# Norms between two engines, ScalarE tables requested ahead of waits, and pooling handed over bank by bank, in a two-block fp32 model kernel

## The chip, the core and the metric

The kernel runs on one core of a Trainium2 chip. TensorE multiplies matrices into the eight banks of PSUM, VectorE (DVE) and ScalarE (ACT) work on tiles in SBUF and PSUM, GpSimd (POOL) helps in the second block, and SyncE (SP) issues the transfers of the weights. The metric is the time of one execution on the device in microseconds; lower is better.

## What is computed

A batch of one, 256 tokens of 1024 fp32 numbers, passes a two-layer block and then a second block. Cut to the parts around the change:

```python
def rms_norm(x, g, eps=1e-6):
    return x * rsqrt(mean(x * x, -1) + eps) * g

# first block
h = h + even_mixer(rms_norm(h, ln_mix_even), ...)   # differential attention + gated recurrence
h = h + swiglu(rms_norm(h, ln_ffn_even), ...)       # hidden width 2816
h = h + pool_mixer(rms_norm(h, ln_mix_odd), pool_w, pool_scale)   # windows 2, 4, 8, 16
h = h + moe_swiglu(rms_norm(h, ln_ffn_odd), ...)    # 8 experts of 3584, top 2
x = rms_norm(h, final_g)

# second block: mod_* are six vectors from the condition c, ctx a second sequence of 256 tokens
hx = rmsnorm(x, g_mix) * (1 + mod_x[1]) + mod_x[0]
hc = rmsnorm(ctx, g_mix) * (1 + mod_c[1]) + mod_c[0]
x = x + mod_x[2] * hybrid_mixer(hx, hc, ...)        # gated delta net and a gated recurrence in two directions
hx = rmsnorm(x, g_ffn) * (1 + mod_x[4]) + mod_x[3]
x = x + mod_x[5] * hier_moe(hx, ...)                # 4 groups of 8 experts of 512, top 2 in the best group
out = rmsnorm(x, g_final)
```

## The kernel before

Every engine has its own program, written out in order, and they meet at semaphores: `done(...)` counts a semaphore up at the end of an instruction and makes the same engine wait for it, `wait_ge(*at(name, n))` waits for the n-th signal of that name. The order of each engine is the order of the code. Names such as `poolT_copied` or `gates_ready` share one semaphore with others of their stage (the table SHARED), which is why the order below shows `ve_mixer1` or `pe_hgrn2`.

The 256 tokens are two tiles of 128 (t = 0, 1), held in `res[:, t, :]` with tokens on the partitions. For projections the features must be on the partitions: TensorE transposes 16 blocks of 128x128 of the scaled rows `xn` into four PSUM banks (`norm_T`), each bank with two of the eight feature chunks for all 256 tokens, and the banks are copied to `hTx`.

There are nine norms, numbered 0 to 8: before the mixer (0), the FFN (1), pooling (2), of the context (3), before the first experts (4), final of block one (5), before the second mixer (6), before the second experts (7), and the output (8). In each, ScalarE squares the two token tiles with a running sum (`sumsq`), VectorE divides and adds eps (`ms_ready`), ScalarE computes exp(-0.5 ln(ms)) in two instructions that need two different activation tables (`rstd_ready`), and VectorE scales both tiles into `xn` (L1309, `xn_ready`). For norms 5 and 8 VectorE multiplies by the gain row as a second pass (L1647, L1950). After the transposes VectorE empties the banks: `norm_copy` (L1315, norms 0, 1, 4) with one 128x512 multiply a bank, `norm_modulate` (L1325, norms 3, 6, 7) with one 128x256 multiply-add for each chunk.

A ScalarE function needs its table in place. In the kernel before no load is written in the code; the compiler puts an ACT_TABLE_LOAD directly ahead of the first instruction of another table. Where that instruction waits for two semaphores, one of the two waits moves onto the load.

Pooling (L959 to L973): TensorE multiplies the rows of norm 2 with a band matrix into banks 0 to 3 (one signal `pool_ready`), VectorE copies them with a gain (L1610, `poolT_copied`), TensorE multiplies with `pool_w` (`pool_y`), VectorE multiplies by `pool_scale` (L1617) and adds to `res` (L1621).

The large weights stream through a ring of six slots of 2 MB on SyncE's queue, in the order of `plan`; each load waits until the slot's last reader is done. The first experts (`units_round`) work in 56 units of up, transpose and down (L705, L712, L726), the second (`pairs_round`) in 16 pairs of experts (L790, L806). Here a load of the next pair waits for `m2_g`, `m2_u` and `m2_dn` of the one before.

In the second mixer, L1201 and the lines behind it are one direction of the gated recurrence (d = 0, 1): ScalarE's sigmoids, VectorE's preparation (L1814 to L1820), Ln on ScalarE, VectorE's running sums (L1828), Exp on ScalarE, TensorE's transposes of the decayed keys, ScalarE's copy of them to `kdTok`, the product for the state, VectorE's copy of it (L1841), and then eight levels in which all engines hand on. In front of norm 7 VectorE adds the mixer's output to `res` (L1906, L1908), makes eight diagonal matrices (L1911, `dg_ready`), and a one-element memset (L1913) signals `res_ready`. For that signal GpSimd waits too: it then issues the loads of the router's columns and biases (L2353 to L2356), for which TensorE waits ahead of the router product (`router2_in`, all four).

## Time and profile before

| what | value |
|---|---|
| median of 3 runs | 2769.88 us (2763.08 to 2772.87) |
| profiled execution | 2766.34 us, its span 2764.5 us |
| TensorE busy | 2476.4 us, 90% of the span |
| VectorE, ScalarE, GpSimd busy | 631.5, 369.1, 150.4 us |
| table loads on ScalarE | 65, 83.4 us together |
| moved by the weights' queue | 666.91 MB |

The span by stages:

| stretch, us | stage | TensorE busy, us | granted clock | DMA share |
|---|---|---|---|---|
| 0 to 176 | norm 0, projections, attention | 126.9 | 0.88 | 0.72 |
| 176 to 218 | recurrent gates, output projection | 29.6 | 0.84 | 0.55 |
| 218 to 231 | norm 1 | 3.9 | 0.61 | 0.44 |
| 231 to 458 | FFN | 227.0 | 1.00 | 0.33 |
| 458 to 537 | norms 2 to 4, pooling, routing | 38.0 | 0.68 | 0.37 |
| 537 to 1521 | first experts | 967.7 | 0.99 | 0.95 |
| 1521 to 1551 | norms 5 and 6, context keys | 21.1 | 0.89 | 0.51 |
| 1551 to 1856 | projections and delta net | 270.5 | 0.94 | 0.00 |
| 1856 to 2192 | gated recurrence, branches, output | 298.8 | 0.97 | 0.25 |
| 2192 to 2237 | norm 7, routing | 17.9 | 0.66 | 0.43 |
| 2237 to 2740 | second experts | 472.2 | 0.98 | 0.98 |
| 2740 to 2764.5 | norm 8, store | 2.7 | 0.62 | 0.12 |

The granted clock is the share of TensorE's full 2.4 GHz that it ran at, so 0.5 is 1.2 GHz. In the rows of the timeline the first number is the start, the second how long, and the bracket at the end names how long the engine was idle before and what released it.

### The profile page before, as it was taken

The page shows a single profiled execution, that of the slowest core. Times are in us where ns is not written, and L with a number is a line of the kernel's source. Part 1 is how long each engine was busy: PE and PEld are TensorE (multiplying, and loading weights), DVE is VectorE, ACT ScalarE, POOL GpSimd, SP SyncE. Part 2 cuts the span into 40 slices and gives each one's busy share as a digit, 9 for nine tenths or more (in the row PEclk, how much of TensorE's full clock was granted, in tenths as well). Part 3 has the DMA queues.
Part 4 walks back from the last instruction along what each step waited for, and adds up shares of the span by engine and source line. Part 5 has one row for each costly group of instructions (what it writes and reads, how often), then busy time and mean ns, then how long its engine had stood idle before and what let it go on. Part 6 is the DMA issues. An engine that isn't in the chain of part 4 may idle for free.

```text
span 2764.5 us, 52752 instructions
## 1 busy us (share of the span) xinstructions
PE 2476.4 (90%) x24386; PEld 1594.9 (58%) x24386; DVE 631.5 (23%) x1191; ACT 369.1 (13%) x596; POOL 150.4 (5%) x140
## 2 busy tenths in 40 slices
PE   6768998599999999999999879999789879999996
PEld 5536775456556656655566658895567534443442
DVE  1441001401010100100010346741542232222223
ACT  1121001100000000000000232312241101011011
POOL 1000000000000000000000005530210000000000
PEclk9889999799999999999999989999999989999998
DMA  8574332399989999998999200013021449999994
GB/s 290 183 273 145 131 137 87 116 393 352 393 309 393 351 355 344 351 394 313 393 351 367 84 1 1 1 44 139 31 92 61 161 186 399 399 399 402 402 398 166
DMA packets 273243, 676.24 MB, mean 245 GB/s; under 512 B 5875, under 2 KB 9422, under 8 KB 268814
## 3 DMA queue, kind: packets, MB, share of 16 engines
q1 hardware_dynamic: 270608, 666.91, 64.3%
q0 software_dynamic: 2112, 6.04, 0.6%
q8 instruction: 184, 3.01, 0.4%
q14 instruction: 21, 0.17, 0.0%
q10 hardware_dynamic: 318, 0.10, 0.0%
HBM read 671.98 MB, written 1.05 MB: 243 GB/s over the span
## 4 chain that ended last, share of the span: by engine, by line
PE 59%; DMA 10%; DVE 5%; ACT 3%; issue 2%; SPq 2%; POOL 1%; DVEq 0%; ACTq 0%
PE ps L705 21%; PE ps L615 14%; PE ps L726 11%; DMA ring<-in_w_exp_up 10%; PE ps L790 5%; ACT arena L1956 2%; SPq L562 2%; PE ps L1074 1%; PE ps L1086 1%; PE ps L1084 1%; PE ps L712 1%; PE ps L688 1%; POOL arena L2348 1%; ACT L1956 1%; PE ps L806 1%
## 5 line engine op out<-in xcount | busy, mean ns | idle before, releaser
L705 PE MATMUL ps<-ring,arena 128*32 128x256 f32 x10752 | 597.8, 382 | 16.9 <-issue 15.6
L705 PEld LDWEIGHTS ps<-ring,arena 128*32 128x32 f32 x10752 | 349.0, 111 | 249.7 <-issue 32.3
L615 PE MATMUL ps<-hT,ring 128*128 128x256 f32 (+1 forms) x1792 | 443.9, 409 | 22.2 <-ACT arena L1956 7.3
L615 PEld LDWEIGHTS ps<-hT,ring 128*128 128x128 f32 x1792 | 346.9, 194 | 124.7 <-issue 69.4
L1956 ACT ACTIVATE arena<-ps 128x384 f32<-128x384 f32 (+5 forms) x311 | 165.2, 552 | 1826.6 <-PE ps L705 576.2
L726 PE MATMUL ps<-ring,arena 128*32 128x256 f32 x5376 | 300.5, 379 | 0.0
L790 PE MATMUL ps<-ring,arena 128*64 128x512 f32 x1024 | 235.2, 614 | 31.7 <-DMA ring<-in_w_exp_up 28.8
L726 PEld LDWEIGHTS ps<-ring,arena 128*32 128x32 f32 x5376 | 173.9, 110 | 115.3 <-issue 1.3
L1403 DVE TENSOR_TENSOR arena<-arena,ps 128x384 f32<-128x384 f32 x56 | 31.0, 554 | 825.3 <-ACT arena L1956 825.3
L790 PEld LDWEIGHTS ps<-ring,arena 128*64 128x64 f32 x1024 | 81.0, 141 | 182.7 <-issue 182.7
L615 PE MATMUL ps<-arena 128*128 128x128 f32 (+1 forms) x1048 | 132.2, 287 | 20.6 <-DVE arena L1431 7.5
L615 PEld LDWEIGHTS ps<-arena 128*128 128x128 f32 x1048 | 128.6, 203 | 22.5 <-DVE arena L1431 7.6
L806 PE MATMUL ps<-ring,arena 128*64 128x512 f32 x512 | 113.4, 595 | 0.0
L2292 POOL TENSOR_TENSOR arena<-arena,table 128x512 f32<-128x512 f32 x24 | 32.1, 1355 | 1442.1 <-ACT arena L1956 1415.3
L1956 ACT ACT_TABLE_LOAD x65 | 83.4, 1283 | 197.6 <-PE ps L615 84.7
L1454 DVE TENSOR_TENSOR arena<-arena,ps 128x512 f32<-128x512 f32 x16 | 11.0, 687 | 303.8 <-PE ps L790 303.8
L954 PE MATMUL ps<-ring,arena 128*128 128x512 f32 x176 | 79.0, 592 | 0.0
L1956 ACT ACTIVATE arena<-arena 128x512 f32<-128x512 f32 (+3 forms) x72 | 59.5, 864 | 137.2 <-DVE arena L1662 32.2
L806 PEld LDWEIGHTS ps<-ring,arena 128*64 128x64 f32 x512 | 35.3, 137 | 66.6 <-issue 66.6
L615 PE MATMUL ps<-ring,arena 128*128 128x512 f32 (+2 forms) x176 | 61.2, 502 | 12.3 <-DVE arena L1309 9.7
L646 PE MATMUL ps<-table,arena 128*128 128x128 f32 x96 | 20.0, 396 | 57.4 <-DVE arena L1309 57.4
L777 PE MATMUL ps<-arena 128*128 128x512 f32 x136 | 62.9, 605 | 1.1 <-ACT arena L1956 1.1
(353 smaller groups left out, 1808.0 us busy)
## 6 DMA issues: line engine op xcount, KB each, us to landing
ring<-in_moe_wg SPq DMA_DIRECT2D x56, 2048.0 KB, 11.4
ring<-in_moe_wu SPq DMA_DIRECT2D x56, 2048.0 KB, 16.4
ring<-in_moe_wd SPq DMA_DIRECT2D x56, 2048.0 KB, 17.2
ring<-in_w_exp_gate SPq DMA_DIRECT2D x32, 2048.0 KB, 17.5
ring<-in_w_exp_up SPq DMA_DIRECT2D x32, 2048.0 KB, 18.8
ring<-in_w_exp_down SPq DMA_DIRECT2D x32, 2048.0 KB, 15.0
ring<-in_w_in SPq DMA_DIRECT2D x13, 2048.0 KB, 10.7
ring<-in_w_ada SPq DMA_DIRECT2D x12, 2048.0 KB, 10.5
```

The source lines that it names most:

```text
L562: sp.dma_start(dst, w[2 * p + j, :, :].rearrange(rows_, p=P))\
L615: last = mm(outp, l, r, start=(i == 0), stop=(i == n - 1))
L688: last = mm(ps[:, 4 + q, t * S:(t + 1) * S], un_GcT[32 * q:32 * q + 32, 1 - b, 3 * t + r, :], ysb[32 * q:32 * q + 32, r * S:(r + 1) * S], ...
L705: last = mm(flat[32 * q:32 * q + 32, S * r:S * r + S], x_[:, k, 32 * r:32 * r + 32], gu[:, :, k, q * P:(q + 1) * P], start=(k == 0), stop= ...
L726: last = mm(flat[32 * q:32 * q + 32, 3 * 512 + S * r:3 * 512 + S * r + S], un_actT[:, c, r, :], d_[:, c, q * S:(q + 1) * S], start=(j == 0 ...
L777: last = mm(ps[:, (6 if t == 0 else 4) + c, :], GcT[:, 1 - b, t, :], ysb[:, c * 512:(c + 1) * 512], start=True, stop=True)
L790: last = mm(ps[64 * j:64 * j + 64, part, :], x_[:, k, 64 * j:64 * j + 64], weights(3 * j + part, KC)[:, k, :], start=(k == 0), stop=(k == ...
L806: last = mm(ps[64 * j:64 * j + 64, 4 + h_, :], pr_actT[:, c, 64 * j:64 * j + 64], weights(3 * j + 2, 4)[:, c, h_ * 512:(h_ + 1) * 512], st ...
L954: last = mm(ps[:, 4 + 2 * t + c, :], actb[:, (n - 1) % 4, t * P:(t + 1) * P], d_[:, j, c * 512:(c + 1) * 512], start=(n == 1), stop=(n == ...
L1403: V.tensor_tensor(un_act, un_sg, up_, ALU.mult).then_inc(inc("m1_act"), 1)
L1956: return nc.scalar.activation(*a, **k)
L2292: G.tensor_tensor(WK[g][d][2 + l % 2], WK[g][d][1], rep(level_mask(l, d == 0), 4), ALU.mult)\
```

## The change

Six things change.

- **Loads are written out.** `functions(names)` issues a table load at a chosen place, 27 in all, none inside a loop. Mostly it stands right behind the last instruction of the table before and ahead of the next wait. The compiler still adds a load wherever the table in place is not the one needed, so Exp behind Ln keeps its own. Two of them stand ahead of a plain copy: Ln before `mod_rows` in the attention, Exp before the copy to `kdTok` in the second direction.
- **Squares start at the first tile.** `res_half` signals that tile 0 of `res` is complete, and the square of tile 0 waits for that alone. In front of norm 8 and after norm 5 VectorE works tile by tile for this.
- **Scaling is shared.** VectorE scales tile 0, ScalarE tile 1 (`xn_act`); TensorE waits for both. In norms 5 and 8 VectorE scales and multiplies by the gain in one pass per tile (`norm_result`), and the output is stored tile by tile.
- **Transposed banks are shared.** VectorE empties banks 0 and 2, ScalarE banks 1 and 3 (`gained`, `hT_act`, `hTc_act`).
- **Pooling is signalled bank by bank**, four signals each for `pool_ready`, `poolT_copied` and `pool_y`; TensorE's second product runs group by group instead of tile by tile, and VectorE finishes the first half of the columns before the second.
- **In front of norm 7** the eight diagonal matrices move ahead of the wait for the output projection, and the memset goes.

```diff
@@ SyncE, end @@
-            sp.wait_ge(*at("result", 1))
-            sp.dma_start(out[0].rearrange("(t p) d -> p t d", p=P), res[:, :, :]).then_inc(inc("out_stored"), 16)
-            sp.wait_ge(*at("out_stored", 16))
+            for t in range(NT):
+                sp.wait_ge(*at("result", t + 1))
+                sp.dma_start(out[0, t * P:(t + 1) * P, :], res[:, t, :]).then_inc(inc("out_stored"), 16)
+            sp.wait_ge(*at("out_stored", 16 * NT))
@@ TensorE, pooling @@
-            last.then_inc(inc("pool_ready"), 1)
-            pe.wait_ge(*at("poolT_copied", 1))
+                if c % 2:
+                    last.then_inc(inc("pool_ready"), 1)
             w = take("poolw")
-            for t in range(NT):
-                for g in range(4):
+            for g in range(4):
+                pe.wait_ge(*at("poolT_copied", g + 1))
+                for t in range(NT):
                     last = chain(ps[:, 4 + 2 * t + g // 2, (g % 2) * S:(g % 2 + 1) * S],
                                  [(poolT[:, 2 * g + k, t * P:(t + 1) * P], w[:, 2 * g + k, :]) for k in range(2)])
-            last.then_inc(inc("pool_y"), 1)
+                last.then_inc(inc("pool_y"), 1)
@@ VectorE, norms @@
-                for t in range(NT):
-                    last = V.tensor_scalar(xn[:, t, :], src[:, t, :], rstd[:, t:t + 1], None, ALU.mult)
-                done(last, "xn_ready")
+                done(V.tensor_scalar(xn[:, 0, :], src[:, 0, :], rstd[:, 0:1], None, ALU.mult), "xn_ready")
+            def norm_result(i, row, names):
...
+                for t in range(NT):
+                    done(V.scalar_tensor_tensor(res[:, t, :], res[:, t, :], rstd[:, t:t + 1], row, ALU.mult, ALU.mult), names[t])
             def norm_copy(i, gain):
-                for b in range(4):
+                for b in (0, 2):
...
-                for c in range(KC):
+                for c in (0, 1, 4, 5):
@@ VectorE, in front of norm 7 @@
+            for c in range(8):
+                last = V.tensor_scalar(dg2[:, c, :], ident, mod[:, 40 + c, 0:1], None, ALU.mult)
+            done(last, "dg_ready")
             ve.wait_ge(*at("grow_ready", 1))
...
-            for c in range(8):
-                last2 = V.tensor_scalar(dg2[:, c, :], ident, mod[:, 40 + c, 0:1], None, ALU.mult)
-            done(last2, "dg_ready")
-            done(V.memset(lams[:, 7:8], 0.0), "res_ready")
+                    if n and t == 0:
+                        last.then_inc(inc("res_half"), 1)
+            done(last, "res_ready")
@@ ScalarE @@
+            def functions(names):
+                nc.scalar.preload_act_table_set(names)
+            def norm(i, src, needs, scaled=True):
                 for t in range(NT):
+                    ac.wait_ge(*at(*needs[t]))
                     last = act(xn[:, t, :], src[:, t, :], ACT.Square, accum_out=ss[:, t:t + 1])
                 done(last, "sumsq")
                 ac.wait_ge(*at("ms_ready", i + 1))
                 done(act(lnv, ms, ACT.Ln))
                 done(act(rstd, lnv, ACT.Exp, scale=-0.5), "rstd_ready")
+                if scaled:
+                    act(xn[:, 1, :], src[:, 1, :], ACT.Copy, scale=rstd[:, 1:2]).then_inc(inc("xn_act"), 1)
+            def gained(dst, gain, name, shift=None):
+                for b in (1, 3):
+                    ac.wait_ge(*at("xnT_ready", 4 * nT[0] + b + 1))
+                    for c in (2 * b, 2 * b + 1):
+                        x_, g_ = ps[:, b, (c % 2) * S:(c % 2 + 1) * S], gain[:, c:c + 1]
+                        if shift is None:
+                            last = act(dst[:, c, :], x_, ACT.Copy, scale=g_)
+                        else:
+                            last = act(dst[:, c, :], x_, ACT.Identity, scale=g_, bias=shift[:, c:c + 1])
...
+            functions(SIG)
             ac.wait_ge(*at("gelu_in", 1))
...
+            functions(EXP)
             ac.wait_ge(*at("log_a", 1))
...
+            functions("sqrt_and_others")
             ac.wait_ge(*at("one_minus", 1))
...
-            norm(1)
+            functions(LN)
+            norm(1, res, [("res_half", 1), ("res_ready", 1)])
+            gained(hTx, colA("ln_ffn_even", 0, 8), "hT_act")
+            functions(SILU)
...
+            functions(LN)
             ac.wait_ge(*at("hTc_ready", 1))
-            norm(4, res, ("res_ready", 3))
+            norm(4, res, [("res_half", 3), ("res_ready", 3)])
...
                     done(act(gd0, ps[:, 6:8, :].rearrange("p b (h q) -> p (b h) q", h=2), ACT.Sigmoid), "gate_sig")
+                    functions(EXP)
                 ac.wait_ge(*at("kdT_ready", d + 1))
```

ScalarE from the square root of the recurrent gates to the FFN. `ve_mixer1`, `res_ready`, `res_half`, `ms_ready` are VectorE's signals, `ac_mixer1`, `sumsq`, `ac_step`, `rstd_ready` its own, `xnT_ready` and `gu_ready` TensorE's. Before:

```order
L1956 ACTIVATE arena,small<-res 128x1024 [waits res_ready,ac_mixer1]
L1956 ACTIVATE arena,small<-res 128x1024
L1956 ACT_TABLE_LOAD [waits ms_ready]
L1956 ACTIVATE small<-small 128x2 [waits sumsq]
L1956 ACT_TABLE_LOAD
L1956 ACTIVATE small<-small 128x2 [waits ac_step]
L1956 ACT_TABLE_LOAD [waits gu_ready]
L1956 ACTIVATE arena<-ps 128x256 [waits rstd_ready]
```

Now:

```order
L1981 ACT_TABLE_LOAD [waits ac_mixer1]
L1973 ACTIVATE arena,small<-res 128x1024 [waits res_half]
L1973 ACTIVATE arena,small<-res 128x1024 [waits res_ready]
L1973 ACTIVATE small<-small 128x2 [waits ms_ready,sumsq]
L1973 ACT_TABLE_LOAD
L1973 ACTIVATE small<-small 128x2 [waits ac_step]
L1973 ACTIVATE arena<-res,small 128x1024 [waits rstd_ready]
L1973 ACTIVATE hT<-ps,pA 128x256 [waits xnT_ready]
L1973 ACTIVATE hT<-ps,pA 128x256
L1973 ACTIVATE hT<-ps,pA 128x256 [waits xnT_ready]
L1973 ACTIVATE hT<-ps,pA 128x256
L1981 ACT_TABLE_LOAD
```

The load with the wait for the mean is gone from between the squares and Ln and stands ahead of the squares; the scaling of one tile and four chunks of the transposed banks have come to ScalarE.

TensorE in pooling: the band product and the product with `pool_w`. `ve_mixer1` is VectorE's copy of the pooled banks, `loaded1` and `loaded2` the two weights. Before:

```order
L615 MATMUL ps<-ring,arena 128x256 [waits loaded1,xn_ready]
L615 MATMUL ps<-ring,arena 128x256 x15
L615 MATMUL ps<-ring,arena 128x256 [waits loaded2,ve_mixer1]
L615 MATMUL ps<-ring,arena 128x256 x15
L646 MATMUL ps<-table,arena 128x128 [waits xn_ready]
```

Now:

```order
L616 MATMUL ps<-ring,arena 128x256 [waits loaded1,xn_act,xn_ready]
L616 MATMUL ps<-ring,arena 128x256 x15
L616 MATMUL ps<-ring,arena 128x256 [waits ve_mixer1,loaded2]
L616 MATMUL ps<-ring,arena 128x256 x3
L616 MATMUL ps<-ring,arena 128x256 [waits ve_mixer1]
L616 MATMUL ps<-ring,arena 128x256 x3
L616 MATMUL ps<-ring,arena 128x256 [waits ve_mixer1]
L616 MATMUL ps<-ring,arena 128x256 x3
L616 MATMUL ps<-ring,arena 128x256 [waits ve_mixer1]
L616 MATMUL ps<-ring,arena 128x256 x3
```

One wait for all four banks has become a wait for each, ahead of four products.

ScalarE in the second direction of the gated recurrence, from the sigmoid of the gates to the first levels. The copy of 128x1024 into arena is that to `kdTok`. Before:

```order
L1956 ACT_TABLE_LOAD [waits pe_hgrn2]
L1956 ACTIVATE hT<-ps 128x4x256 [waits ac_hgrn2]
L1956 ACTIVATE arena<-ps 128x1024 [waits pe_hgrn2,ac_hgrn2]
L1956 ACT_TABLE_LOAD [waits Wd_ready]
L1956 ACTIVATE arena<-arena 128x512 [waits ac_hgrn2]
```

Now:

```order
L1973 ACT_TABLE_LOAD [waits pe_hgrn2]
L1973 ACTIVATE hT<-ps 128x4x256 [waits ac_hgrn2]
L1981 ACT_TABLE_LOAD [waits ac_hgrn2]
L1973 ACTIVATE arena<-ps 128x1024 [waits pe_hgrn2]
L1973 ACTIVATE arena<-arena 128x512 [waits Wd_ready,ac_hgrn2]
```

The load for Exp and the copy to `kdTok` have changed places.

## Rows read from the trace of the kernel before

**Rows 1.** Chain that ended last: start us, us, what; first and second experts

```profile
567.12 10.50 PE ps L705 x192
...
2316.53 19.79 DMA ring<-in_w_exp_up
```

**Rows 2.** Groups by cost: busy, mean ns of one, idle before

```profile
L1956 ACT ACT_TABLE_LOAD x65 | 83.4, 1283 | 197.6 <-PE ps L615 84.7 <-DVE arena L1662 31.3 <-DVE arena L1535 18.3
```

**Rows 3.** Timeline of norm 1: start us, us, engine, instruction, [idle before, releaser]

```profile
219.24 1.06 ACT L1956 ACTIVATE arena<-res 128x1024 f32<-128x1024 f32 x1 [24.34 <-DVE res L1588]
...
221.78 1.28 ACT L1956 ACT_TABLE_LOAD   x1 [0.35 <-DVE small L1306]
223.07 0.20 ACT L1956 ACTIVATE small<-small 128x2 f32<-128x2 f32 x1
...
224.89 1.42 DVE L1309 TENSOR_SCALAR arena<-res,small 128x1024 f32<-128x1024 f32 x2 [3.20 <-ACT small L1956]
226.37 3.68 PE L646 MATMUL ps<-table,arena 128*128 128x128 f32 x16 [8.54 <-DVE arena L1309]
```

**Rows 4.** Timeline of the recurrent gates

```profile
181.29 3.02 ACT L1956 ACTIVATE arena<-ps,pA 128x256 f32<-128x256 f32 x8
...
201.27 16.55 PE L934 MATMUL ps<-ring,hT 128*128 128x512 f32 x32 [12.18 <-DVE hT L1584]
```

**Rows 5.** Timeline after norm 0: bank copies and the first projection

```profile
23.07 2.48 DVE L1315 TENSOR_TENSOR hT<-ps,pA 128x512 f32<-128x512 f32 x4
...
25.61 29.52 PE L615 MATMUL ps<-hT,ring 128*128 128x256 f32 x128 [3.31 <-DVE hT L1315]
```

**Rows 6.** Timeline of the softmax of the first query tile

```profile
116.01 1.28 ACT L1956 ACT_TABLE_LOAD   x1 [18.34 <-DVE arena L1535]
...
120.83 1.28 ACT L1956 ACT_TABLE_LOAD   x1
...
122.22 0.66 PE L901 MATMUL ps<-table,arena 128*128 128x128 f32 x4 [2.14 <-DVE arena L1541]
```

**Rows 7.** Timeline of pooling

```profile
480.24 7.17 PE L615 MATMUL ps<-ring,arena 128*128 128x256 f32 x32 [2.64 <-DVE arena L1610]
...
487.55 2.49 DVE L1617 TENSOR_TENSOR ps<-ps,arena 128x512 f32<-128x512 f32 x4 [7.37 <-PE ps L615]
...
492.59 0.17 DVE L1306 TENSOR_SCALAR small<-small 128x2 f32<-128x2 f32 x1
```

**Rows 8.** Norm 6: timeline, then busy time of engines, PEclk, DMA share, GB/s

```profile
1546.06 1.91 PE L646 MATMUL ps<-table,arena 128*128 128x128 f32 x16
1546.77 3.71 DVE L1325 TENSOR_SCALAR hT<-ps,small 128x256 f32<-128x256 f32 x8 [2.18 <-PE ps L646]
1550.53 57.05 PE L615 MATMUL ps<-hT,ring 128*128 128x256 f32 x192 [2.57 <-DVE hT L1325]
...
1550.00:1560.00 10.00, 9.47 (x36) 8.06 (x37) 1.82 (x6) 0.00 (x0) 0.00 (x0) 0.83 0.01 2
```

**Rows 9.** Timeline of TensorE, gated recurrence, first and second direction

```profile
1951.26 1.94 PE L1201 MATMUL ps<-table,arena 128*128 128x128 f32 x8 [5.17 <-DVE arena L1835]
...
2054.45 2.05 PE L615 MATMUL ps<-arena 128*128 128x128 f32 x16 [2.63 <-ACT arena L1956]
```

**Rows 10.** Timeline of norm 7, and the landing of GpSimd's last router load (L2356)

```profile
2194.35 1.65 DVE L1911 TENSOR_SCALAR arena<-table,small 128x128 f32<-128x128 f32 x8
...
2198.80 0.55 POOL L2356 DMA_DIRECT2D arena<-in_b_router_exp  x1
...
2208.55 3.73 PE L615 MATMUL ps<-arena,hT 128*128 128x36 f32 x32
...
DMA to landing us min/median/max: 9.6/9.6/9.6
```

**Rows 11.** Timeline of the end: the multiply by the final gain

```profile
2756.97 2.36 DVE L1950 TENSOR_TENSOR res<-arena 128x1024 f32<-128x1024 f32 x2
```

**Rows 12.** The page: moved by the transfers in 40 equal slices

```profile
GB/s 290 183 273 145 131 137 87 116 393 352 393 309 393 351 355 344 351 394 313 393 351 367 84 1 1 1 44 139 31 92 61 161 186 399 399 399 402 402 398 166
```

More of the change, by code:

```diff
@@ L1643, in _ @@
             done(V.memset(lams[:, 7:8], 0.0), "res_ready")
[L1644 removed]
             ve.wait_ge(*at("fgrow_in", 16))
[L1646 to L1648 removed]
+            norm_result(5, fgrow, ("res_half", "res_ready"))
             norm(6)
```

107 lines of the change are left out of this document (70 added, 37 removed).

## The prediction, made before the changed kernel ran

> **What bounds the kernel now.** I read the chain that ended last first. In the first expert stage (537 to 1521 us) it is TensorE alone: units of 10.50 and 5.18 us follow each other, and SyncE's queue waits for TensorE, not the reverse. In the paired experts (2237 to 2740 us) it is the DMA queue: each pair waits some 20 us for its up weights [rows 1]. The first load of the next pair is asked for when a pair's gate product is done, so both stages are of fixed length and move as a whole: whatever comes earlier ahead of them comes earlier at the end. Neither has a norm in it. The change works on the stretches between, where engines hand one tile back and forth. Before it 65 table loads of 1.283 us ran [rows 2]; what counts is which of them someone waited for.
>
> Norm 1 shows the pattern [rows 3]. ScalarE squares both token tiles, VectorE makes the mean, a load goes by (221.78), then Ln, a second load, Exp; VectorE scales both tiles (1.42 us for the two), TensorE transposes from 226.37 after 8.54 us idle, VectorE empties the banks. I look at each such place for the event that comes last.
>
> **The change, part by part.** Savings are of the path, against the profiled execution.
>
> *Norm, in common.* The order of ScalarE has the mean's wait now on Ln and the load ahead of the squares: 1.28 us off where that stood in an idle wait. The load between Ln and Exp stays. Scaling: before, 1.42 us and two hand-overs between Exp's end and TensorE, 1.58 in all. Now ScalarE scales tile 1 itself; a 128x1024 ScalarE pass took 1.06 us [rows 3], and VectorE's single tile (0.71) is done earlier. With one hand-over some 1.18: 0.4 off. The transposed banks: ScalarE needs 0.378 us for each 128x256 with a column operand (3.02 over 8) [rows 4], two for a bank and a little more for the last, some 0.87; VectorE took 0.62 for a bank (2.48 over 4) [rows 5], 0.69 alone. The last bank comes after TensorE's last transpose in both kernels, so for a gain copy this costs 0.2.
>
> *Norm 0.* 1.28 + 0.4. Here VectorE began its four copies (2.48 us) only when the columns were there, with all banks full [rows 5]; two banks on ScalarE take 1.7, about 0.77 off with hand-overs. Sum 2.45. The first weights were asked for at the start, and nothing else holds the projections.
>
> *Softmax, first query tile.* Exp's load at 116.01 follows VectorE's subtraction; it now stands behind the copy of gb, long before: 1.28. Ln's load ran ahead of its wait already (120.83, right behind a copy): 0. TensorE was idle for 2.14 us before the transposes that wait, so 1.28 fits [rows 6].
>
> *Recurrent gates.* TensorE waits 12.18 us for this branch [rows 4]. Three loads stand in it (before Sigmoid, Exp, Sqrt), each now under VectorE's or TensorE's work: 3.84.
>
> *Norm 1.* 1.28 + 0.4 - 0.2, and one addition less ahead of the first square (0.62, a quarter of 2.49 [rows 7]): 2.1. *Norm 2* feeds the band products directly: 1.28 + 0.4 + 0.95 (two of four additions, 1.24, now beside a square of 1.06): 2.65.
>
> *Pooling.* TensorE's 2.64 us idle before 480.24 goes, as the second product begins on bank 0 while bank 3 is being emptied: 2.64. Behind it VectorE multiplied and added four times each, 4.98 us from 487.55 until norm 3's mean at 492.59 [rows 7]. Half is now under TensorE's second half: 2.4. Norm 3 then saves 1.28 + 0.4 + 0.15: 1.85. *Norm 4* gains no load: its preload is queued behind ScalarE's own bank copies of norm 3 and in front of the squares that wait for just these; +1.28 -1.28, 0.4 - 0.2 remain: 0.2.
>
> *Norms 5 and 6.* TensorE's k product of the context held the transposes: their row at 1546.06 has no idle before it. So what the two norms save themselves is worth 0. After them VectorE took 3.71 us for eight shifts; shared, the last bank is ready 1.1 us after the last transpose (1546.06 + 1.91): 1549.05 against 1550.53, 1.45 [rows 8]. In the 10 us from 1550 the granted clock was 0.83, that is 3.4 us at 1.2 instead of 2.4 GHz after 2.57 us of idle: 1.7 us lost. With 1.1 us idle I take it back; after 2.64 us idle at 480.24 the 32 products ran at 0.22 us each [rows 7], the pace at which the clock is full. Bounds 0 and 1.7.
>
> *Second block.* First direction: two loads (before Ln and before Exp) go, but VectorE's four copies wait for a TensorE product that ends 5.17 us before 1951.26; 2.8 of it remain: 2.35. Second direction: its loads lie beside TensorE's next projections, except one. The preload of Exp now stands ahead of ScalarE's copy for which TensorE waits at 2054.45 [rows 9]; before, it stood behind it, beside TensorE. That costs 1.3: the state product, VectorE's copy of it and the whole level loop are queued behind. Sum 1.05. The Ln and Sigmoid preloads behind it lie under three gate projections: 0. If the shorter gap keeps the clock up at 1951, up to 2.4 more; I take 0.
>
> *Norm 7.* The eight diagonal products (1.65 us) leave the path, tile 0 is squared earlier (about 0.9), 1.28 and 0.4: 4.3. But the router product also needs four small transfers that GpSimd issues on the same release. The last was issued at 2198.80 and landed 9.6 us later, at 2208.4, and the product began at 2208.55: two waits ended together [rows 10]. GpSimd's release moves by the diagonal products and little else. So 2.0; bounds 0 (landing set by the load of the weights in flight) and 4.3.
>
> *End.* Whole-tensor steps become tiles: a square less, some waits more, 0.5; 1.28; scale and gain were 1.42 + 2.36, now two passes of 1.18 (half of 2.36 [rows 11]): 1.3. The store's second half is 0.5 MB; at 402 GB/s, the highest slice [rows 12], that is 1.3 us less, bounds 0 and 1.3, taken 1.0. Sum 4.1.
>
> Sum: 2.45 + 1.28 + 3.84 + 2.1 + 2.65 + 2.64 + 2.4 + 1.85 + 0.2 + 1.45 + 1.7 + 1.05 + 2.0 + 4.1 = 29.7 us. Profiled execution: 2766.34 (span 2764.5, 1.8 around it) - 29.7 = 2736.6. The median of the runs lies 3.5 above it, and the forecast is against the median: 2769.88 - 29.7 = 2740.2.
>
> A load takes its row's time and no more: the one at 221.78 lasts 1.28 us and Ln starts at 223.07 [rows 3]. The Trainium skill (ScalarE: Activation LUTs, What ACT_TABLE_LOAD costs) puts every switch at 1283 ns and a drain of 1380 ns besides, some 2.66 us. The trace agrees with the first and shows nothing of the second; with it the sum would be some 46.
>
> **Rivals.** *A switch costs twice as much.* If something outside the rows belonged to each load, the 12 counted at 1.28 would be worth twice that: 15.4 more, 2725. The close start of Ln behind its load speaks against it: 0.03. (The Trainium skill's figure on that page would make it 16.6 more and 2723.6.)
>
> *The two engines hinder each other.* ScalarE and VectorE now read the same tile or neighbouring banks at once. If each pass took as long as both in turn, the scaling would lose its 0.4 and 0.7 more at seven norms (7.7 us) and the banks some 1.5: gain 20.5, 2749. No row shows the two at once on one source. 0.11.
>
> *The loads don't move in time.* If loads put ahead of the wait still ran behind it, the 15.4 us of the 12 stay: gain 14.3, 2756. The load at 120.83 ran in an open wait, against it: 0.04.
>
> *Slower.* Place: each explicit load, 27 of them, nearly all on a path between two engines. If a load made ScalarE stand until everything behind it had been fetched and drained, and this was not hidden by the wait, each would have to cost 1.1 us net to eat the 29.7, and 1.4 to make the kernel slower by 0.3%; at twice its row, 27 x 2.57 = 69 with nothing hidden, less the 29.7, it is 2809. Only a load that is queued ahead of work (norm 4, second direction) can do that, and I count two. 0.02.
>
> *Forecast* with its small open terms: 0.80.
>
> **How the numbers follow.** Range: the bounds of norm 7 (-2.0, +2.3), store (-1.0, +0.3), clock (-1.7, +2.4) and the hindering rival (-10) give gains of 20 to 35; the runs of before lie 7 below to 3 above their median. That makes 2730 to 2751. Some 0.3% (8.3 us) is what a measurement can tell. Faster than that: forecast, double cost, hindering and most of the unmoved loads, 0.94; within it 0.04; slower 0.02.
>
> **What would show it.** In the changed profile: Ln 0.3 us after the mean in every norm; TensorE idle of about 6.3 us (8.54) before norm 1's transposes, 8.3 (12.18) before the gates' product, none before the pooled product; the second direction's state product 1.3 us later after its gate sigmoid; the router product some 2 us after the hidden matrix of norm 7 is ready, behind the last small transfer; expert stages of unchanged length. I am wrong if these lengths change, if ScalarE's scaling pass is well over 1.1 us, or if clock dips appear where there were none.

## The result, and the profile after

The changed kernel takes **2737.16 us** (median of 4 runs, 2734.26 to 2737.68), the kernel before beside it 2767.31 (2763.08 to 2772.87): ratio 0.9886, 95% interval 0.9868 to 0.9903. The forecast was 2740.2 with a range of 2730 to 2751. The profiled execution took 2734.26 us (span 2732.5), that is 32.0 us less span than before, against 29.7 forecast.

To see where the 32.0 us came from I took pairs of the same event in both timelines (a product's start, a norm's mean) and noted how much earlier each is now. The difference from one pair to the next belongs to what lies between.

| what | forecast, us | by the two traces, us | earlier by then, us |
|---|---|---|---|
| norm 0 | 2.45 | 2.73 | 2.73 |
| first two projections (30.74 us now, [rows 5]) | 0 | -1.23 | 1.50 |
| softmax, first query tile | 1.28 | 1.31 | 2.81 |
| rest of attention | 0 | 0.46 | 3.27 |
| recurrent gates | 3.84 | 3.94 | 7.21 |
| norm 1 | 2.1 | 2.28 | 9.49 |
| norm 2 | 2.65 | 2.64 | 12.13 |
| pooling | 5.04 | 4.59 | 16.72 |
| norm 3 | 1.85 | 1.53 | 18.25 |
| norm 4 | 0.2 | 0.61 | 18.86 |
| first router, gather | 0 | -2.23 | 16.63 |
| first experts | 0 | 0.67 | 17.30 |
| norm 6 | 1.45 | 1.32 | 18.62 |
| clock dip behind it | 1.7 | 1.68 | 20.30 |
| delta net | 0 | 0.17 | 20.47 |
| recurrence, first direction | 2.35 | 2.65 | 23.12 |
| recurrence, second direction | -1.3 | -2.38 | 20.74 |
| norm 7 | 2.0 | 1.31 | 22.05 |
| second routing | 0 | 0.61 | 22.66 |
| second experts | 0 | 4.30 | 26.96 |
| end | 4.1 | 5.04 | 32.0 |

The terms that had a forecast sum to 29.7 there and 29.3 here. The rows without one sum to 2.8, and singly they reach -2.2 and +4.3. The table compares one execution of each kernel. Its row of the first two projections shows how far that carries: ten kernels of this study have the same 2.44 us of idle time ahead of these 128 products, and the products took 29.40 to 29.55 us in seven of them and 30.68 to 30.83 in three, the changed kernel among the three. So the -1.23 is no fixed part of the change. The rows of norm 3 and norm 4 end where the transposes begin; the banks emptied behind those count in the row below.

Norm 1 in the changed kernel, the answer to [rows 3] (timeline: start us, us, engine, instruction, [idle before, releaser]):

```profile
213.74 0.17 DVE L1316 TENSOR_SCALAR small<-small 128x2 f32<-128x2 f32 x1 [1.73 <-ACT arena L1973]
214.00 0.20 ACT L1973 ACTIVATE small<-small 128x2 f32<-128x2 f32 x1 [0.37 <-DVE small L1316]
214.23 1.28 ACT L1973 ACT_TABLE_LOAD   x1
215.52 0.20 ACT L1973 ACTIVATE small<-small 128x2 f32<-128x2 f32 x1
215.76 1.15 ACT L1973 ACTIVATE arena<-res,small 128x1024 f32<-128x1024 f32 x1
215.83 0.75 DVE L1318 TENSOR_SCALAR arena<-res,small 128x1024 f32<-128x1024 f32 x1 [1.92 <-ACT small L1973]
217.05 3.30 PE L648 MATMUL ps<-table,arena 128*128 128x128 f32 x16 [6.36 <-ACT arena L1973]
...
219.03 0.84 ACT L1973 ACTIVATE hT<-ps,pA 128x256 f32<-128x256 f32 x2 [2.12 <-PE ps L648]
```

Ln starts 0.26 us after the mean; the load ahead of it is gone. One load remains between Ln and Exp. The two engines scale a tile each at the same time, and TensorE's idle time is 6.36 us where it was 8.54. ScalarE empties a bank in 0.84.

TensorE at the recurrent gates' consumer, in pooling and at the two norms behind it (timeline of the changed kernel; [rows 4] and [rows 7] are its counterparts):

```profile
194.06 16.63 PE L937 MATMUL ps<-ring,hT 128*128 128x512 f32 x32 [8.25 <-DVE hT L1600]
...
456.12 17.06 PE L616 MATMUL ps<-ring,arena 128*128 128x256 f32 x64 [7.07 <-DVE arena L1318]
479.17 3.65 PE L648 MATMUL ps<-table,arena 128*128 128x128 f32 x16 [6.00 <-ACT arena L1973]
490.80 3.65 PE L648 MATMUL ps<-table,arena 128*128 128x128 f32 x16 [7.98 <-ACT arena L1973]
495.42 6.96 PE L616 MATMUL ps<-arena,hT 128*128 128x8 f32 x32 [0.98 <-issue]
```

Three loads are out of the gates' wait (12.18 to 8.25), and the two pooled products are one run of 64. The last row is the surprise: the same 32 products of the router took 4.33 us before. The view of busy times by stretches gives the reason, first the kernel before, then the changed one (columns: us, busy us and count of PE, PEld, DVE, ACT, POOL, then PEclk, DMA share, GB/s):

```profile
514.00:518.50 4.50, 4.33 (x32) 4.24 (x32) 0.04 (x1) 0.00 (x0) 0.00 (x0) 0.84 0.00 0
```

```profile
495.40:502.40 7.00, 6.96 (x32) 6.89 (x32) 0.00 (x0) 0.00 (x0) 0.00 (x0) 0.50 0.00 0
```

The granted clock was 0.50 (1.2 GHz) from first to last of these products, and 0.84 on average over the same products in the kernel before.

### The profile page after: what moved, and what is told of

It reads as the page before. It is cut to its first block, busy times and chain, and to the rows that moved or that the text cites. A ratio compares the mean times of both kernels' runs of the same rounds, so it can differ in the third digit from the quotient of the medians.

```text
span 2732.5 us, 52735 instructions
## 1 busy us (share of the span) xinstructions
PE 2478.2 (91%) x24386; PEld 1600.1 (59%) x24386; DVE 615.7 (23%) x1163; ACT 374.7 (14%) x616; POOL 150.8 (6%) x140
## 4 chain that ended last, share of the span: by engine, by line
PE 75%; DMA 11%; DVE 6%; ACT 3%; issue 2%; SPq 2%; POOL 1%; DVEq 0%; POOLq 0%; ACTq 0%
PE ps L616 24%; PE ps L707 22%; PE ps L728 11%; DMA ring<-in_w_exp_up 10%; PE ps L792 5%; PE ps L958 3%; ACT arena L1973 2%; SPq L562 2%; PE ps L1083 1%; PE ps L1095 1%; PE ps L1093 1%; PE ps L714 1%; PE ps L690 1%; POOL arena L2417 1%; ACT L1973 1%
## 5 line engine op out<-in xcount | busy, mean ns | idle before, releaser
L707 PE MATMUL ps<-ring,arena 128*32 128x256 f32 x10752 | 597.4, 382 | 16.7 <-issue 15.4
L1617 DVE TENSOR_TENSOR arena<-arena,ps 128x256 f32<-128x256 f32 x22 | 9.3, 421 | 213.2 <-ACT arena L1973 213.2
## 6 DMA issues: line engine op xcount, KB each, us to landing
ring<-in_w_in SPq DMA_DIRECT2D x13, 2048.0 KB, 10.5
ring<-in_w_ada SPq DMA_DIRECT2D x12, 2048.0 KB, 10.5
```

The source lines that it names most:

```text
L707: last = mm(flat[32 * q:32 * q + 32, S * r:S * r + S], x_[:, k, 32 * r:32 * r + 32], gu[:, :, k, q * P:(q + 1) * P], start=(k == 0), stop= ...
```

## Experiments: whose gain is it?

Medians are compared with the kernel before measured on the same chip in the same batch; "earlier" figures are from the profiled executions, as in the table above. The changed kernel ran in a batch of its own. The intervals of these ratios are 10 to 13 us wide, so where two medians lie 5 us apart or less, the traces and not the medians carry the argument. In every kernel the line numbers differ by a few. Those derived from the changed kernel say so.

### The loads alone

The kernel before, with the 27 explicit loads at the places where the change has them, and nothing else of it:

```diff
+            def functions(names):
+                nc.scalar.preload_act_table_set(names)
...
+            functions(LN)
             norm(1)
+            functions(SILU)
             for n in range(FFN // P):
```

> The kernel before with nothing but the explicit table loads at the places where the change has them. By the terms of the forecast: norm 0 1.28, softmax 1.28, gates 3.84, norms 1 to 4 5.13 (norm 4 gains its load here, since ScalarE has no bank copies of norm 3 in front of it), end 1.28, first direction of the recurrence 2.6, second direction -1.3 and, if TensorE's clock falls after the longer idle as it did in the changed kernel, another -1.6; norm 7 0, since GpSimd's transfers are asked for at the same point. Sum 14.1, or 12.5 with the clock: 2753 to 2755 us. If a load on the path were worth twice its row: gain 26, 2741. If the loads did nothing and sharing were the whole gain: 2764 to 2768.

Measured: 2753.1 us against 2765.9, ratio 0.9947 (0.993 to 0.9965); the profiled span is 11.5 us shorter. The forecast's 1.28 for each counted load fits; twice the price does not. Norm 4 gained its load here (1.32), as it should without bank copies in front. The second direction's product started after 3.92 us idle and took 3.18 us instead of 2.05, and the first router's product took 7.00. The second pooled product (TensorE's timeline) ran like this, against 7.17 us after 2.64 us idle before [rows 7]:

```profile
473.41 8.60 PE L615 MATMUL ps<-ring,arena 128*128 128x256 f32 x32 [2.65 <-DVE arena L1610]
```

The idle time in front of it is the same, and its granted clock was 0.83 where it had been 1.00. So the length of the last idle row does not settle the clock by itself.

### Everything but the loads

```diff
             def functions(names):
-                nc.scalar.preload_act_table_set(names)
+                pass
```

> The changed kernel without its 27 explicit loads; each load then stands where it is needed, behind the wait. By the terms: 11 loads come back onto the path (norms 0 to 3 and 8 five, softmax one, gates three, first direction two) = 14.1 us, and the second direction's copy of kdTok is again ahead of Exp's load: -1.3, and -1.6 if its clock dip goes too. So 11.2 to 12.8 slower than the changed kernel, 2748 to 2750, that is a gain of 17 to 19 on the kernel before. If loads are worth twice: 2762. If sharing were the whole gain: 2737.

Measured: 2747.3 us, ratio 0.9924 (0.9906 to 0.9941), 18.6 below the kernel before. With the 12.8 of the loads alone that is 31.4, near the 30.2 of both together; by the profiled spans it is 11.5 and 16.5, and 32.0 together. Within a few us the two parts add, and neither needs the other. The larger part of the gain comes from what is not loads: the sharing, the hand-over by tiles, pooling and the new order in front of norm 7.

### What a load costs on the path

The changed kernel, with two needless loads in every norm:

```diff
                 ac.wait_ge(*at("ms_ready", i + 1))
+                functions(SILU)
+                functions(LN)
                 done(act(lnv, ms, ACT.Ln))
```

> The changed kernel with two needless loads (another set, and Ln's again) between the mean and Ln in all nine norms. It measures what a load on the path costs. At the row's 1.28 us: 2.57 for each of norms 0 to 4 and 8, those of norm 7 under the wait for the small transfers, those of 5 and 6 under the k product as far as it reaches (0 to 5.1): 15.4 to 20.5 slower, 2753 to 2758. With the drain that the Trainium skill (ScalarE: Activation LUTs, What ACT_TABLE_LOAD costs) puts beside each, 2.66 in all: 32 or more, 2769 and above, and a gap of 1.38 us behind each load in the trace. If loads overlapped with what waits, 2737.

Norm 1 in its timeline, ScalarE:

```profile
215.18 2.57 ACT L1981 ACT_TABLE_LOAD   x2 [0.35 <-DVE small L1316]
217.76 0.20 ACT L1973 ACTIVATE small<-small 128x2 f32<-128x2 f32 x1
```

Two loads last 2.57 us together and Ln follows at once. Nothing like a second price stands beside them: the Trainium skill's 1380 ns of drain (ScalarE: Activation LUTs, What ACT_TABLE_LOAD costs) is not in these rows. Each of norms 0, 1, 2 and 4 became 2.45 to 2.58 longer up to its Ln. The total, 2747.5 us (ratio 0.9936, 0.9912 to 0.996), is only 10.3 above the changed kernel, under the 15.4 expected; the profiled span is 10.9 longer. In norm 7 the loads hid behind GpSimd's transfers, as expected. The trace shows most of what is missing in products that ran faster than in the changed kernel: the first router's in 5.17 us and not in 6.96, the first projections in 29.55 and not in 30.74, the pooled ones in 16.01 and not in 17.06, the second router's in 3.73 and not in 4.42.

### Scaling on VectorE alone

The changed kernel; TensorE's and ScalarE's `xn_act` go too:

```diff
-                done(V.tensor_scalar(xn[:, 0, :], src[:, 0, :], rstd[:, 0:1], None, ALU.mult), "xn_ready")
+                for t in range(NT):
+                    last = V.tensor_scalar(xn[:, t, :], src[:, t, :], rstd[:, t:t + 1], None, ALU.mult)
+                done(last, "xn_ready")
```

> The changed kernel with VectorE scaling both token tiles again, as before, ScalarE none. By the forecast (1.18 us from Exp's end to TensorE shared, 1.58 alone): 0.4 us slower at norms 0 to 4 and nothing at norms 5 to 8: 2.0 us, 2739. If the two engines hindered each other on one source (the hindering rival), taking the sharing away gives 0.7 us back at each: 3 us faster, 2734.

TensorE's idle time ahead of norm 1 and ahead of norm 3's transposes, now (timeline):

```profile
215.87 3.67 PE L647 MATMUL ps<-table,arena 128*128 128x128 f32 x16 [6.61 <-DVE arena L1317]
...
480.95 3.50 PE L647 MATMUL ps<-table,arena 128*128 128x128 f32 x16 [6.25 <-DVE arena L1317]
```

Against 6.36 and 6.00 with sharing: 0.25 each (0.29 at norm 2, 0.33 at norm 4), not the forecast's 0.4, since ScalarE's pass took 1.15 us where a pass without the column operand had taken 1.06. VectorE's tile took 0.75 us beside ScalarE and also 0.75 in the kernel before, where it scaled alone. So two engines reading one source at once do not hinder each other by more than 0.1 us, and that rival has fallen. The total was 2741.4 us (ratio 0.991, 0.9887 to 0.9932), 4.2 above the changed kernel, and the profiled span is 7.3 longer. Only some 1.5 of that stands in the waits of norms 0 to 4. The largest part is again a clock: the first product of the second experts took 16.94 us at a granted clock of 0.82, and 13.95 at 1.00 in the changed kernel.

### Banks on VectorE alone

The changed kernel with `norm_copy` and `norm_modulate` over all banks again, and `gained` gone with its waits:

```diff
-                for b in (0, 2):
+                for b in range(4):
...
-            gained(hTx, gA, "hT_act", mod[:, 0:8, 0])
```

> The changed kernel with all four transposed banks emptied by VectorE again. By the forecast: norm 0 0.8 slower, norms 1 and 4 0.2 faster each, norm 3 0.15 slower, norm 6 1.45 slower and the clock dip behind it back, 1.7; norm 4 also gets its preload out of the queue behind ScalarE's copies of norm 3, 1.3 faster. Sum 2.0 to 2.4 slower: 2739. If the engines hindered each other on neighbouring banks, sharing is worth 1.5 less: 2737.5. If the load at norm 4 was not held by those copies: 2740.5.

Norm 6 (timeline; the first view ends at 1550 us and cuts its last row, which in full is 57.05 us for 192 products; the last row is the changed kernel's):

```profile
1526.94 1.91 PE L648 MATMUL ps<-table,arena 128*128 128x128 f32 x16
1527.65 3.71 DVE L1335 TENSOR_SCALAR hT<-ps,small 128x256 f32<-128x256 f32 x8 [7.72 <-PE ps L648]
1531.42 18.77 PE L616 MATMUL ps<-hT,ring 128*128 128x256 f32 x71 [2.56 <-DVE hT L1335]
...
1531.91 55.33 PE L616 MATMUL ps<-hT,ring 128*128 128x256 f32 x192 [1.24 <-ACT hT L1973]
```

In the changed kernel both engines need 1.9 us there, and the product starts after 1.24 us idle. From the last expert to the gated recurrence the changed kernel gained 3.21 us, this one 0.07: the 1.45 and the 1.7 of the clock dip behind it are both real, and the dip comes and goes with this idle time (57.05 us after 2.56 and 2.57 us of it, 55.33 after 1.24). From norm 3's Ln to norm 4's this kernel gained 1.60 where the changed one gained 0.52: the load that queued behind ScalarE's bank copies was indeed that norm's loss. Total: 2737.9 us (ratio 0.9901, 0.9877 to 0.9924). In sum the medians show nothing of sharing banks, though it is worth 3 us at norm 6. It gives back 1.1 at norm 4, and here the first router's product took 4.87 us and no longer 6.96.

### Pooling handed over at once

The changed kernel with one signal each for `pool_ready`, `poolT_copied`, `pool_y`, and TensorE's and VectorE's loops of before:

```diff
-                if c % 2:
-                    last.then_inc(inc("pool_ready"), 1)
+            last.then_inc(inc("pool_ready"), 1)
```

> The changed kernel with the pooling signalled once for all four banks, as before; norms as changed. By the terms: TensorE idle again 2.64 us before the second product, and VectorE's four products and four sums all behind it, 2.4 us: 5.0 slower than the changed kernel, 2742. If the clock at the second product is what the change really moved (one run of 64 products took 17.06 us, the two halves of before 9.35 and 7.17), the two halves show 16.5 us again and the net is 4.5. If the overlap brought nothing: 2737.

```profile
457.43 8.63 PE L616 MATMUL ps<-ring,arena 128*128 128x256 f32 x32 [7.07 <-DVE arena L1317]
468.71 7.17 PE L616 MATMUL ps<-ring,arena 128*128 128x256 f32 x32 [2.65 <-DVE arena L1629]
```

Measured: 2741.8 us (ratio 0.9915, 0.9895 to 0.9935), 4.6 above the changed kernel. These two rows (TensorE's timeline) span 18.45 us, the single run 17.06: of the 2.65 us idle only 1.4 came back to TensorE. The changed kernel's 64 products ran at a granted clock of 0.61 over their first 8 us and of 1.00 behind that, and were 1.3 us longer than these two halves. VectorE's part came in full.

## Experiments: the terms that were off

### Second direction of the recurrence

Forecast -1.3, traced -2.38. In the changed kernel (timeline, ScalarE and TensorE):

```profile
2028.72 1.02 ACT L1973 ACTIVATE hT<-ps 128x1024 f32<-128x1024 f32 x1
2029.76 1.28 ACT L1981 ACT_TABLE_LOAD   x1
2031.06 1.02 ACT L1973 ACTIVATE arena<-ps 128x1024 f32<-128x1024 f32 x1
...
2032.13 3.62 PE L616 MATMUL ps<-arena 128*128 128x128 f32 x16 [3.92 <-ACT arena L1973]
```

The load stands ahead of the copy of `kdTok`, as the forecast had it, and TensorE is idle for 3.92 us and not 2.63. But the 16 products behind took 3.62 us, and 2.05 before [rows 9]. I moved the load alone:

```diff
-                    functions(EXP)
                 ac.wait_ge(*at("kdT_ready", d + 1))
                 done(act(kdTok, ...), "kdTok_ready")
+                if d == 1:
+                    functions(EXP)
```

> The changed kernel with one load moved: in the recurrence's second direction the load for Exp stands behind ScalarE's copy of kdTok, no longer ahead of it. My theory: the copy comes 1.28 us earlier after the gate's sigmoid, TensorE's idle before the state product falls from 3.9 to 2.6 us, the 16 products take 2.05 us and not 3.62: 2.8 us in all, so 2734.4. If the clock dip came from something else, the products still take about 3.6 us and the gain is 1.3. If the load were hidden behind a later wait: 0.

```profile
2030.43 1.02 ACT L1973 ACTIVATE arena<-ps 128x1024 f32<-128x1024 f32 x1
2031.48 1.28 ACT L1981 ACT_TABLE_LOAD   x1
...
2031.51 2.05 PE L616 MATMUL ps<-arena 128*128 128x128 f32 x16 [2.63 <-ACT arena L1973]
```

Both came back: 1.29 idle and 1.57 of products. So one load ahead of a hand-over cost 2.9 us, less than half of it its own row. Over all fourteen kernels of this study, the one before among them, the product took 2.05 us in the five where the idle row reads 2.63, and 3.17 to 3.62 in the nine where it reads 3.92. The median, 2735.0 us (ratio 0.9875, 0.9852 to 0.9899), is 2 us lower, which by itself could be noise; this kernel's profiled second expert stage was as long as before the change, which the next part is about.

### Norm 7 and the second experts

Forecast 2.0 for norm 7, traced 1.31, capped as foretold. In the changed kernel (timeline of GpSimd's last router load, TensorE's router product):

```profile
2176.36 0.55 POOL L2425 DMA_DIRECT2D arena<-in_b_router_exp  x1
...
2186.50 4.42 PE L616 MATMUL ps<-arena,hT 128*128 128x36 f32 x32 [2.49 <-DMA arena<-in_b_router_exp]
```

The tile that the loads go to is free as soon as the gated branches are summed:

```diff
-            po.wait_ge(*at("res_ready", 6))
+            po.wait_ge(*at("mg_ready", 1))
```

> The changed kernel with GpSimd's transfers for the second router (weights, biases and the row of the last gain) asked for when the gated branches are summed, some 24 us earlier, and no longer when the residual is ready. Theory (the wait for the last small transfer capped norm 7): the router product starts right behind ScalarE's last bank, near 1.1 us after the last transpose; in the changed kernel that was at 2183.1 and the product at 2186.5, so up to 3.4 us: 2733.8, unless the paired stage's own length moves, which it did by up to 4.3 us between earlier runs. If something else held the product, 0; if the transfers take the queue from the output weights, the y product starts later: slower by 1 to 3.

```profile
2176.38 3.65 PE L648 MATMUL ps<-table,arena 128*128 128x128 f32 x16 [7.38 <-ACT arena L1973]
2179.82 2.30 PE L1293 MATMUL ps<-arena,table 128*128 128x512 f32 x4
2181.95 3.66 PE L616 MATMUL ps<-arena,hT 128*128 128x36 f32 x32
```

The product follows without idle time and takes 3.66 us instead of 4.42; from norm 7's Ln to the routing's exponential 3.4 us came back, what was expected. Median 2730.8 us (ratio 0.9875, 0.9853 to 0.9897), 6.4 below the changed kernel's by the medians and 3 by the ratios.

The second experts were taken as of fixed length, and the changed kernel has them 4.3 us shorter. The head of the stage is its first products, up to the first load that they wait for; the foot is the last product behind the last load. The chains that ended last there, the kernel before and then the changed kernel (start us, us, what):

```profile
2237.85 15.39 PE ps L790 x64
...
2281.92 2.94 SPq L562
2284.96 19.87 DMA ring<-in_w_exp_up
...
2694.19 19.82 DMA ring<-in_w_exp_up
2714.15 8.78 PE ps L790 x32
```

```profile
2215.19 13.95 PE ps L792 x64
...
2259.71 19.98 DMA ring<-in_w_exp_up
...
2668.93 19.81 DMA ring<-in_w_exp_up
2688.88 7.09 PE ps L792 x32
```

From 2284.96 to 2694.19 it is 409.2 us, and in the changed kernel 409.2: the DMA-bound middle is fixed, as forecast. The head is not. Its first product ran in 15.39 and 13.95 us by the clock that the routing left behind, and SyncE's queue held the second load 1.16 less. Nor is the foot: every third or so of the products in between takes 8.5 to 8.8 us instead of 7.10, which costs nothing there, and in the kernel before the last one was such. Head and foot over the kernels: 15.39 and 8.78 before, 13.95 and 7.09 changed, 16.91 and 7.09 loads alone, 15.45 and 7.09 no loads, 15.30 and 8.78 with the load behind the copy, 13.95 and 7.09 for the kernel of the next part. The stage's length followed: 502.9, 498.6, 502.2, 500.3, 502.9, 499.2. Two more kernels had a long first product, 16.94 with scaling on VectorE and 16.86 with ten needless transposes (below). So these 4.3 us are no fixed part of the change. What decides which product comes last at the lower clock, and the queue's part, I leave open.

## Beyond the change

### One table set for Ln and Exp

A load stands between Ln and Exp in each norm. The Trainium skill (ScalarE: Activation LUTs, Table sets) names a set that holds both. In the changed kernel, with reloads of the set already in place left out:

```diff
-            EXP, LN, SILU, SIG = "exp_and_others", "natural_log",
+            EXP, LN, SILU, SIG = "natural_log_exp_and_others", "natural_log_exp_and_others",
...
-            functions(EXP)
+            functions("exp_and_others")
             ac.wait_ge(*at("log_a", 1))
```

> The changed kernel with the one table set that holds both Ln and Exp in place of the two sets, so that no load stands between Ln and Exp any more (the Trainium skill, ScalarE: Activation LUTs, Table sets, says that such a set exists), and with loads left out where that set is already in. By the rows: in norms 0, 1, 2, 3 and 8 one load less on the path, 6.4; in norm 4 the queued load too, 2.6; softmax up to 1.3; norm 7 0, since the small transfers end last there; norms 5 and 6 0. Sum 9 to 10.3: 2727 to 2728. If a switch had a price outside its row: 18 or more, 2719. If the loads between Ln and Exp were hidden: 2737.

```profile
213.03 0.44 ACT L1973 ACTIVATE small<-small 128x2 f32<-128x2 f32 x2 [0.36 <-DVE small L1316]
213.50 1.15 ACT L1973 ACTIVATE arena<-res,small 128x1024 f32<-128x1024 f32 x1
```

Norm 1 on ScalarE (timeline): Ln and Exp are one row of 0.44 us. Measured: 2728.8 us (ratio 0.9856, 0.9834 to 0.9878), 8.4 below the changed kernel. Executed loads fell from 54 to 32.

### All together

One set, the load behind the copy, the router's loads early, and the joint set also fetched right behind the sigmoid ahead of the delta net:

```diff
+            functions(LN)                                    # behind the sigmoid for beta
...
-                    functions(EXP)
                 ac.wait_ge(*at("kdT_ready", d + 1))
...
-            po.wait_ge(*at("res_ready", 6))
+            po.wait_ge(*at("mg_ready", 1))
```

> The changed kernel with what the runs showed to be worth it: one table set for Ln and Exp (medians 8.4 apart), the Exp load behind the kdTok copy (2.85 by the trace), the router's transfers earlier (5.3 by the trace), and the joint set also loaded behind the sigmoid ahead of the delta stage, four loads fewer there (0 to 3 on the path). With the transfers early the load between Ln and Exp of norm 7 is on the path too: 1.3. Sum 17.9 to 20.9: 2716 to 2719. If the gains don't add, because each rests on the same idle time: 2722 to 2728.

Measured: **2713.1 us** (2712.6 to 2714.2), ratio 0.9805 (0.9791 to 0.9819); 28 loads are left. That is more than expected: 24.1 below the changed kernel. The delta net's stretch gave most of what the sum had not (from the last expert to the gated recurrence 6.77 us gained, where the changed kernel has 3.21).

### The clock behind a wait

The first router's product ran in 6.96 to 7.00 us in nine kernels and in 4.33 to 5.17 in four (before, no loads, banks on VectorE, two more loads), with 6.9 to 10.5 us idle ahead of the transposes in front of it in these four and 5.3 to 8.3 in the nine. So a shorter wait had not meant a better clock; what put a kernel among the four I leave open. I first gave TensorE ten needless transposes in the waits of norms 1, 2, 4 and 7 of the changed kernel:

```diff
+            def idle_turns(value):
+                pe.wait_ge(*at("res_ready", value))
+                for _ in range(10):
+                    nc.tensor.transpose(ps[:, 7, 0:P], ident, ident)
...
+            idle_turns(3)
             norm_T(3, 4)
```

> The changed kernel with ten transposes of the identity into PSUM bank 7, which nothing reads, on TensorE while it waits for the scaled tiles of norms 1, 2, 4 and 7. They take 2.3 us (0.23 each by the norm's own transposes) inside idle times of 6.4 to 8.0 us, and end before the tiles are there. Theory (the longer products behind a norm are the granted clock after idle time): the 64 pooled products fall from 17.06 towards 14 us, the 32 router products of 6.96 towards 4.4, those of norm 7 from 4.4 towards 3.7; 4 to 6 us in all, 2732. If the length of these products has another cause: 2737. If the clock falls anyway since ten transposes aren't enough, between: 2735. If the added work holds the transposes up: above 2740.

Measured: 2736.4 us (ratio 0.9884, 0.9867 to 0.9902). None of these got faster: 64 pooled products in 17.07 us, 16 transposes of norm 4 in 3.64 after 5.53 us idle, the first router's product at a clock of 0.50. By itself this reads as if idle time were not the cause. But the ten stood at the head of the wait, and 2.4 to 5.5 us of idle time were left behind them. The last kernel adds more of them to the best one, 24, 14, 18 and 14:

```diff
+            idle_turns(1, 24)
             norm_T(1)
...
+            idle_turns(3, 18)
             norm_T(3, 4)
```

> The best kernel so far, with needless transposes of the identity on TensorE that fill nearly all of the waits ahead of the transposes or products of norms 1, 2, 4 and 7 (24, 14, 18 and 14 of them; ten left 2.4 to 5.5 us of idle time and changed no product). If TensorE's clock behind a norm rests on its own idle time, the transposes of the norms (3.65 us for 16) go towards 2.1, the first router's product (6.96 at a granted clock of 0.50) towards 4.3 or below: 4 to 8 us off the 2713.1 of that kernel. If ten changed nothing because idle time is not what the clock follows there, nothing changes: 2713. If they run over into the wait's end: up to 2 us slower.

Norm 4 (TensorE's timeline, the needless transposes in the first row), and the stretches of norm 3's transposes, norm 4's and the router's product:

```profile
471.93 3.92 PE L646 MATMUL ps<-table 128*128 128x128 f32 x18 [1.16 <-DVE hT L1350]
476.04 1.94 PE L653 MATMUL ps<-table,arena 128*128 128x128 f32 x16 [0.18 <-ACT arena L1982]
478.95 3.83 PE L616 MATMUL ps<-arena,hT 128*128 128x8 f32 x32 [0.98 <-DVE hT L1340]
```

```profile
467.10:471.00 3.90, 3.65 (x16) 3.27 (x16) 1.99 (x4) 1.21 (x3) 0.00 (x0) 0.50 1.05 387
475.90:478.10 2.20, 1.94 (x16) 1.74 (x16) 1.21 (x2) 0.93 (x3) 0.00 (x0) 1.00 1.02 408
478.90:482.90 4.00, 3.83 (x32) 3.77 (x32) 0.01 (x1) 0.00 (x0) 0.00 (x0) 0.94 0.01 4
```

Norm 3, which got none, keeps 3.65 us at 0.50; norm 4 has 1.94 at 1.00, and the router's product 3.83. The 64 pooled products took 14.05 us, and 16.59 without the needless transposes. Measured: **2708.9 us** (2705.8 to 2710.6), ratio 0.9781 (0.9763 to 0.9798). Its interval just overlaps that of the kernel without them, so the 4.2 us between the medians are weak evidence; the profiled spans lie 7.4 us apart and the rows above show where. The clock behind a norm does rest on TensorE's idle time. Ten transposes at the head of a wait bought nothing; the same number at its end was not tried. This is the fastest kernel of the study, 2.2% below the kernel before (2.0% for the best one without the needless transposes).

## Why the prediction was right

**What bounds the kernel.** Right for the first experts (0.67 us off). For the second only the DMA-bound middle is fixed; its head and foot run by TensorE's clock. That was the step that failed: "both stages are of fixed length", and it gave 4.3 us that I had not counted. Of my three signs of being wrong two appeared, this length and clock dips where there were none; ScalarE's scaling pass, 1.15 us, stayed near its 1.1.

**Loads.** Right: 1.28 each, by the trace where they stand alone (softmax 1.31, gates 3.94 for three), by the loads alone (12.8 us in all, 12.5 expected with the dip) and by the two added ones. The queued load at norm 4 and the one ahead of `kdTok` were both found where the forecast put them.

**Scaling and banks.** Mechanism right, sizes off: 0.25 to 0.33 for 0.4, and ScalarE's bank takes 0.84 us for a gain but 1.02 with gain and shift. Norm 3's row is 0.3 short: half of that is the scaling, and the other half, its banks, counts in the row below. Norm 6 was 0.1 short for the slower banks.

**Pooling.** 4.59 for 5.04: the idle time of 2.64 was taken as won whole, but the 64 products in one run took 0.5 us longer than the two halves of before together (17.06 and 16.52).

**Clock.** The dip behind norm 6 was taken back in full, as I chose. Three dips that I hadn't are new: 1.2 us in the first projections, which most kernels with the same 2.44 us of idle time there don't show, 1.6 in the second direction and 2.6 in the first router's product. My reason, that after 2.64 us idle the pooled products had run at full pace, was too weak: with the loads alone the same product took 8.60 us after 2.65 us idle. It was not asked of the 3.92 that my own term produced either.

**Norm 7 and end.** The cap by the small transfers was right and 0.7 tighter than taken; 0.4 of that is the last transfer, which landed 10.0 us after its issue and not 9.6. At the end scale and gain gave 1.2 (1.3 forecast), tiles 1.1 (0.5), the store 1.45 (1.0; it bounded at 1.3): from VectorE's last row to the end of the span it is 3.7 us where it was 5.2.

**Range.** Its lower gain of 20 takes the hindering rival alone; with the bounds of norm 7, store and clock beside it the sum would be 15.

So the close hit owes something to luck: outside the forecast terms -3.5 and +6.2 us met, and that they left only 2.8 was not foreseen.

## What to carry to other kernels

Fetch the next table as soon as the last instruction of the old one is issued, but behind any ScalarE copy for which another engine waits; and first ask whether one set holds both functions, which here took another 8.4 us off. A term that lengthens or shortens TensorE's wait has a second price, the clock of what comes behind: read the granted clock of that stretch. Here filling paid where it left 0 to 1.5 us of idle time ahead of the work, and not where it left 2.4 to 5.5. A stage that is bound by DMA has a head and a foot that are not.

## What the runs showed of the hardware that I had not expected

- Sixteen 128x128 transposes took 3.2 to 3.7 us in norms 0, 1, 3, 4 and 7 wherever TensorE had waited for them, at a granted clock of 0.50 in norm 4 of the changed kernel, and 1.94 when it had been kept busy. In norm 6, where a product runs right up to them, they took 1.91 in every kernel. No engine's idle row shows that price.
- Ten needless transposes in a wait of 7.07 us left the 64 products behind it at 17.07 us (17.06 without them); fourteen in one of 5.79, with no idle time behind them, brought 14.05.
- Two ScalarE passes over 128x256, one behind the other, took 0.84 us with one column operand each and 1.02 with two each, 0.09 more for each pass and operand. The Trainium skill (ScalarE: Activation LUTs, What ACT_TABLE_LOAD costs) puts each such operand at about 93 ns; these rows agree.
- Loads follow each other and their function within 0.02 us.
